# Attention of the second tower: one head after another, or two heads side by side

## What is computed

```python
def diff_attend(q1, q2, k1, k2, v, lam):
    scale = DIFF_QK_DIM ** -0.5
    p1 = jax.nn.softmax(jnp.einsum('bqhd,bkhd->bhqk', q1, k1).astype(jnp.float32) * scale, axis=-1)
    p2 = jax.nn.softmax(jnp.einsum('bqhd,bkhd->bhqk', q2, k2).astype(jnp.float32) * scale, axis=-1)
    p = (p1 - lam * p2).astype(v.dtype)
    return jnp.einsum('bhqk,bkhv->bqhv', p, v)

def gqa_attend(q, k, v):
    B, Q, H, d = q.shape
    qg = q.reshape(B, Q, GQA_KV_HEADS, GQA_GROUP, d)
    s = jnp.einsum('bqgrd,bkgd->bgrqk', qg, k).astype(jnp.float32) * (d ** -0.5)
    p = jax.nn.softmax(s, axis=-1).astype(v.dtype)
    return jnp.einsum('bgrqk,bkgd->bqgrd', p, v).reshape(B, Q, H, d)

def attn_heads(q1, q2, qb, k1, k2, va, kb, vb, lam, lam_init, subln):
    B, Q = q1.shape[:2]
    oa = rms_norm_2(diff_attend(q1, q2, k1, k2, va, lam), subln) * (1 - lam_init)
    ob = gqa_attend(qb, kb, vb)
    return jnp.concatenate([oa.reshape(B, Q, -1), ob.reshape(B, Q, -1)], axis=-1)
```

## Time and profile before

| | us |
|---|---|
| median of three runs | 3231.71 |
| span of the profiled execution | 3245.1 |
| TensorE busy in it | 2922.6 |
| VectorE busy | 1840.6 |
| ScalarE busy | 1181.5 |
| GpSimd busy | 1162.3 |
| attention of the second tower, first score matmul to output projection | 257.9 |

### The profile page before, as it was taken

The page is one execution under the profiler, slowest core; times in us unless marked ns, Lnnn a source line. Parts: engine busy times, 40 slices in busy tenths (PEclk is TensorE's granted clock), DMA queues, the critical chain, the costliest instruction groups (busy, mean ns, idle before and its releaser), DMA issues.

```text
span 3245.1 us, 37354 instructions
## 1 busy us (share of the span) xinstructions
PE 2922.6 (90%) x13432; PEld 2251.8 (69%) x13432; DVE 1840.6 (57%) x2520; ACT 1181.5 (36%) x1710; POOL 1162.3 (36%) x545
## 2 busy tenths in 40 slices
PE   0989898999999789989999699999899999789997
PEld 0855476888888645567777487555688878668886
DVE  7849677554646438589999753744541331454133
ACT  3325523121222425432223532354452433355242
POOL 5289212323332284134444221000344443234442
PEclk9999999999999899999999898899999999899999
DMA  6310033322323110135554231100233232123332
GB/s 245 131 65 1 1 120 120 119 100 100 123 97 131 57 65 1 40 136 181 172 179 167 101 133 39 59 1 15 77 96 97 97 104 76 55 78 97 98 97 72
DMA packets 82261, 303.56 MB, mean 94 GB/s; under 512 B 8928, under 2 KB 10464, under 8 KB 81248
## 3 DMA queue, kind: packets, MB, share of 16 engines
q1 hardware_dynamic: 81856, 298.42, 27.1%
q10 hardware_dynamic: 288, 3.55, 0.3%
HBM read 299.83 MB, written 2.10 MB: 93 GB/s over the span
## 4 chain that ended last, share of the span: by engine, by line
PE 74%; DVE 13%; issue 6%; ACT 4%; POOL 1%; DMA 1%; DVEq 0%; SPq 0%; ACTq 0%; POOLq 0%
PE psum L1401 21%; PE psum L1521 14%; PE psum L1118 9%; PE psum L1542 7%; PE psum L1217 5%; PE psum L1191 4%; PE psum L1156 2%; PE psum L1203 2%; PE psum L1138 2%; DVE product_scratch L1685 2%; DVE rstd L1628 2%; PE psum L1309 1%; DVE scratch L1973 1%; DVE scratch L1611 1%; DVE in_lo L1602 1%
## 5 line engine op out<-in xcount | busy, mean ns | idle before, releaser
L537 POOL TENSOR_TENSOR w_lo<-w_raw,w_hi 128x1024 fp32r<-128x1024 f32 x346 | 879.1, 2541 | 2025.6 <-ACT w_hi L611 2025.6
L611 ACT ACTIVATE w_hi<-w_raw 128x1024 fp32r<-128x1024 f32 x346 | 366.6, 1060 | 1222.1 <-PE psum L1401 488.1
L1690 DVE CUSTOM_DVE_ANT_0 mod_w<-mod_w,conditions 128x1024 f32<-128x1024 f32 x176 | 345.2, 1961 | 5.7
L1665 DVE SCALAR_TENSOR_TENSOR residual<-psum,modulation,residual 128x512 f32<-128x512 f32 (+1 forms) x168 | 111.7, 685 | 345.8 <-PE psum L1542 156.9
L1521 PE MATMUL psum<-in_hi,w_hi 128*128 128x512 f32 x672 | 261.6, 389 | 2.0 <-DVE small_w L2132 1.0
L1521 PE MATMUL psum<-in_hi,w_lo 128*128 128x512 f32 x672 | 261.4, 389 | 0.0
L1521 PE MATMUL psum<-in_lo,w_hi 128*128 128x512 f32 x672 | 261.4, 389 | 0.0
L1401 PE MATMUL psum<-hidden_hi,w_hi 128*128 128x512 f32 (+1 forms) x768 | 237.6, 364 | 25.5 <-DVE hidden_lo L1959 25.1
L1191 PE MATMUL psum<-mixer_space 96*128 96x384 f32 (+2 forms) x544 | 225.9, 542 | 17.0 <-DVE mixer_space L1865 10.3
L1401 PE MATMUL psum<-hidden_hi,w_lo 128*128 128x512 f32 (+1 forms) x768 | 236.3, 362 | 0.0
L1401 PE MATMUL psum<-hidden_lo,w_hi 128*128 128x512 f32 (+1 forms) x768 | 234.5, 360 | 0.0
(11 more groups left out here) (237 smaller groups left out, 5759.5 us busy)
## 6 DMA issues: line engine op xcount, KB each, us to landing
w_raw<-stream_dram SPq DMA_DIRECT2D x346, 512.0 KB, 3.8
mod_w<-mods_dram SPq DMA_DIRECT2D x176, 512.0 KB, 3.5
mixer_space<-mods_dram SPq DMA_DIRECT2D x12, 512.0 KB, 10.7
small_w<-small_w_dram SPq DMA_DIRECT2D x2, 2048.0 KB, 11.2
in_hi_space<-dft_x_dram SPq DMA_DIRECT2D x2, 2048.0 KB, 9.1
residual<-tokens_dram ACTq DMA_DIRECT2D x1, 3072.0 KB, 13.2
conditions<-conditions_dram SPq DMA_DIRECT2D x2, 1024.0 KB, 5.8
in_lo_space<-mods_dram SPq DMA_DIRECT2D x4, 512.0 KB, 9.4
```

The source lines that it names most:

```text
L537: nc.gpsimd.tensor_tensor(wlo[:, (j % 2) * 1024:(j % 2 + 1) * 1024], raw3[:, j, :], whi[:, (j % 2) * 1024:(j % 2 + 1) * 1024].bitcast(F32) ...
L611: nc.scalar.activation(whi[:, (j % 2) * 1024:(j % 2 + 1) * 1024], raw3[:, j, :], ACT.Copy).then_inc(hi_ready, 1)
L1665: last = nc.vector.scalar_tensor_tensor(res3[:, m, s0:s1], bank(2 * (t % 2) + b, c1=s1 - s0), M(block_, chunk, m, 1 - b), res3[:, m, s0:s1 ...
L1690: nc.vector.tensor_tensor_reduce(w_tile, w_tile, cvec[:, 0:D], 1.0, 0.0, ALU.mult, ALU.add, dots[:, q:q + 1]).then_inc(mod_done, 1)
```

## The change

`gqa_plan` becomes `pair_plan`: its steps alternate between an even head (side 0, rows 0-63) and the odd head beside it (side 1, rows 64-127), and a group is two heads at 256 queries. A **pair** d is steps 2d and 2d+1, the two sides of one look. There are 16 differential pairs (first and second looks in turn) and 16 grouped pairs, still 64 steps. Slots, buffers and arithmetic are the same; now side 0 always has banks 0-1 and side 1 banks 2-3, and `pt2` has one buffer per side.

The scores of a pair are issued in alternation, and wait for both exponentials of the pair before. Grouped weighted sums alternate between the sides, into the two halves of bank 6's partitions, so that there are eight evictions of 128 partitions in place of sixteen of 64. Differential ones stay apart. The orders of ScalarE and VectorE go by pairs. The modulation tiles stand one in each of the pairs 0 to 11, after the maxima of the next pair. The head norms start at pairs 10, 13, 18 and 21, and the inverse root and the gain are now both in the pair after the start.

```diff
-SUB_AT, SUB_STEP = 33, 7
+SUB_AT = (10, 13, 18, 21)
+DIFF_PV = 8
...
+            for c in range(2):
                 for q0 in (0, 256):
...
+                    group(c, q0, "diff", [(c, c), (2 + c, 2 + c)])
+            for c in range(4):
+                for q0 in (0, 256):
+                    group(c, q0, "gqa", [(4 + c, 4)])
...
+            pair_exp(0)
+            pair_exp(1)
+            for d in range(n_pairs):
+                before = pair_steps[2 * d - 2] if d else None
+                if d and before["last"]:
+                    pair_hi(pair_groups[before["group"]], 0)
+                if d >= 2 and pair_steps[2 * d - 4]["last"] and pair_steps[2 * d - 4]["post"] == "second":
+                    pair_hi(pair_groups[pair_steps[2 * d - 4]["group"]], 1)
+                for i in (2 * d, 2 * d + 1):
+                    pair_ev(i)
+                if d + 1 < n_pairs:
+                    for i in (2 * d + 2, 2 * d + 3):
+                        pair_exp(i)
+                sub_norm(d)
...
+            def pair_scores(d):
+
+                if d:
+                    pe.wait_ge(sa["exped"], 2 * d)
+                for b in (0, 1):
+                    for i in (2 * d, 2 * d + 1):
+                        st = pair_steps[i]
+                        mm = pe.matmul(bank(2 * (i % 2) + b, c1=384), st["q"],
+                                       st["k"][:, 384 * b:384 * b + 384], start=True, stop=True)
+                        if b:
+                            mm.then_inc(sa["scores"], 1)
...
+                for k in range(6):
+                    for side in range(2):
+                        mm = pe.matmul(bank(6, 64 * side, 64 * side + 64, 0, 256),
+                                       v2[:, k, 512 + 64 * side:576 + 64 * side], pt2[side][:, k, :],
+                                       start=(k == 0), stop=(k == 5))
+                mm.then_inc(sa["pv"], 1)
+
+            pair_scores(0)
+            for d in range(n_pairs):
+                pair_turn(2 * d)
+                if d + 1 < n_pairs:
+                    pair_scores(d + 1)
+                if d and pair_steps[2 * d - 1]["last"] and pair_steps[2 * d - 1]["post"] == "second":
+                    pair_pv_diff(2 * d - 1)
+                pair_turn(2 * d + 1)
+                if pair_steps[2 * d]["last"]:
+                    if pair_steps[2 * d]["post"] == "second":
+                        pair_pv_diff(2 * d)
+                    else:
+                        pair_pv_gqa(2 * d)
...
+            for d in range(n_pairs):
+                for i in (2 * d, 2 * d + 1):
+                    pair_weigh(i)
+                if d and pair_steps[2 * d - 1]["last"] and pair_steps[2 * d - 1]["post"] == "plain":
+                    pair_lo(pair_groups[pair_steps[2 * d - 1]["group"]])
+                if d + 1 < n_pairs:
+                    for i in (2 * d + 2, 2 * d + 3):
+                        pair_max(i)
+                if d < MOD_ATT:
+                    mod_tile(m0 + d, d, False)
+                if d == MOD_ATT:
+                    mod_out(m0, MOD_ATT, group, False)
+                sub_norm(d)
```

More of the change, by code:

```diff
@@ new lines, in pair_plan, with group @@
+        def pair_plan():
+            steps, groups = [], []
+            def group(tile, q0, kind, looks):
+                g = len(groups)
+                groups.append(dict(tile=tile, q0=q0, kind=kind))
+                for j in range(2):
+                    for n, (qt, kt) in enumerate(looks):
+                        for side in range(2):
+                            r = slice(64 * side, 64 * side + 64)
+                            steps.append(dict(
+                                group=g, half=j, side=side, last=j == 1 and n == len(looks) - 1,
+                                post="plain" if len(looks) == 1 else ("first", "second")[n],
+                                q=q2[r, qt, q0 + j * P:q0 + (j + 1) * P], k=k2[r, kt, :]))
+            for c in range(2):
+                for q0 in (0, 256):
+                    group(c, q0, "diff", [(c, c), (2 + c, 2 + c)])
+            for c in range(4):
+                for q0 in (0, 256):
+                    group(c, q0, "gqa", [(4 + c, 4)])
+            turns = 0
+            for st in steps:
+                st["t"] = None
+                if st["post"] != "first":
+                    st["t"] = turns
+                    turns += 1
+            pvs = 0
+            for gr in groups:
+                gr["pv"] = [pvs, pvs + (gr["kind"] == "diff")]
+                pvs = gr["pv"][1] + 1
+            return steps, groups
@@ L983, in _ @@
             nc.scalar.activation(coef[:, 0:2], bank(7, c1=2), ACT.Exp).then_inc(s2["lam"], 1)
[L985 to L995, removed]
+            sa = att[2]
@@ new lines, in pv_free, with pair_pv_diff @@
+            def pv_free(e):
+                if e:
+                    pe.wait_ge(sa["pv_hi"], e)
+                if e > DIFF_PV:
+                    pe.wait_ge(sa["pv_lo"], e - DIFF_PV)
+            def pair_pv_diff(i):
+                st = pair_steps[i]
+                gr = pair_groups[st["group"]]
+                h = 2 * gr["tile"] + st["side"]
+                pe.wait_ge(sa["ev"], st["t"] + 1)
+                pv_free(gr["pv"][st["side"]])
+                for k in range(6):
+                    mm = pe.matmul(bank(6, c1=256), v2[:, k, h * P:(h + 1) * P], pt2[st["side"]][:, k, :],
+                                   start=(k == 0), stop=(k == 5))
+                mm.then_inc(sa["pv"], 1)
```

157 lines of the change are left out of this document (103 added, 54 removed).

## The result

Four runs of the changed kernel took 3247.74 to 3258.60 us, median 3252.18; four of the kernel before, beside them, 3229.77 to 3233.35, median 3231.37. The ratio is 1.0065, with a 95% interval of 1.0051 to 1.0080: **slower by 20.8 us, 0.65%**. The forecast was 3255 us.

A forecast was written before the change was run, and what follows sets the result against it. TensorE, busy 90% of the span, was taken as the bound. Stage 279 us at clock 0.75, 21 over 257.9, plus 2 for the projection: +23 on 3231.7, so 3255 us; own range 3241 to 3268, full range 3228 to 3287.

The forecast's parts named there:

- What bounds the stage, and what the loop loses: Second tower's attention: TensorE bounds it; pairs fill both score slots, so scores can't run ahead; 211 us before head norms.
- The four spacings at the full clock: Scores to next pair's scores: first look 4.9, second look with tile 7.2, grouped without weighted sum 5.8, with it 6.8 us.
- Full overlap of the array's row halves: Two heads' scores cost 1.49 us instead of 2.98; with paired weighted sums, TensorE's list shrinks by 69 us.
- Rival 1: Scores overlap less, a pair taking five lengths: stage 295 us at clock 0.75, kernel 3271; chance 0.09.
- The modulation tile on the path: On VectorE in second looks, the tile stands ahead of the weighting and adds 1.20 us, in six pairs.
- Rival 4: Some loop item, say the modulation tile, is hidden; gain and loss cancel within 6 us; chance 0.08.
- The head norms: Four times, VectorE's gain waits for ScalarE's root ahead of both weightings: 25 us for all four at full clock.
- The clock: TensorE pauses in every pair, so the stage's mean granted clock is taken as 0.75, against 0.85 before.
- mixing of 236 and 342 us: New stage's layout at full clock and with every TensorE item doubled, mixed by mean clock: 279 us at 0.75.
- break-even at 0.86: Mean stage clock at which the new stage equals the old; faster above it.
- Rivals 2 and 3: Clock falls to 0.6: stage 314, kernel 3290 us, chance 0.09; clock stays 0.95: stage 243, kernel 3217, chance 0.12.
- The projection's cold start: The output projection after the stage begins at the low clock about half the time: 2 us added.

The follow-up runs named there:

- e9: Kernel before with only the grouped weighted sums of two heads in pairs, and head norms' inverse roots replaced by a copy: 3209.06 us, ratio to before 0.9933.
- e12: Kernel of e6 with the head norms' inverse roots replaced by a copy: 3216.80 us, ratio to before 0.9954.
- e2: Changed kernel with both heads' scores on array rows 0-63, the even head's computed twice: 3330.84 us in its one execution.
- e3: Changed kernel with the even head's score matmuls issued before the odd head's, not in alternation: 3255.87 us, ratio to before 1.0059.
- e5: Changed kernel with VectorE's twelve modulation tiles moved ahead of the next pair's maxima: 3243.80 us, ratio to before 1.0040.
- e1: Changed kernel with VectorE's gain and remainder of each head norm one pair later: 3226.59 us, ratio to before 0.9975.
- e4: Changed kernel with one unused matmul added at the end of pairs without a weighted sum, away from the norms: 3239.47 us, ratio to before 1.0017.
- e6: Changed kernel with the edits of e1 and e5, head norms at pairs 10, 14, 18, 22 and ScalarE's copy later: 3216.23 us, ratio to before 0.9959.
- e7: Kernel before with only the grouped weighted sums of two heads in pairs, scores still one step ahead: 3225.95 us, ratio to before 0.9981.

## Why the prediction was right

- **What bounds the stage, and what the loop loses.** Right. TensorE's list carried the stage before, the one-step lead fed it, and the pairs lost the lead. The four spacings at the full clock were forecast as 4.9, 7.2, 5.8 and 6.8 us; the trace has 5.03, 7.12, 5.80 and 6.81, in the five of 31 pairs that ran wholly at the full clock. That the lead was lost is read from these spacings and from e9 beside e12. No kernel that pairs the scores and keeps a lead ran, so its share of the 81 us is not measured.
- **Full overlap of the array's row halves**, taken from the column case of rows 6. Right: 1.56 us for eight records, and e2 and e3 show it from both sides. Rival 1, five record lengths a pair, is out by the 1.56 us, and by e3. The TensorE list was to shrink by 69 us at the full clock; busy time fell by 64, at a lower clock. The Trainium skill ("TensorE: Matmul & The Clock Gate", Part 3) lets matmuls start only in list order; e3's pair, at 1.57 us with one head wholly ahead of the other, disagrees with it. The Trainium skill ("TensorEngine Tiling (Array Packing)", Key Properties) says that tiles operate independently, and e3 agrees. Rows 6, which the prediction set against list order, decide less: the two projection records belong to one matmul, and the weighted sum starts after the first of them.
- **The modulation tile on the path.** Right in place, too large in size: the sum has 1.2 us for each of six at the full clock, the pairs of e5 show 0.8. Its 9.9 us hold what the clock gave back. Rival 4 is out.
- **The head norms.** Right in place, and one wait of two: VectorE idles 4.02, 5.00, 5.16 and 5.17 us ahead of the gains, about 4 was forecast. The waits ahead of the remainders, 7.4 us, are in no term of the sum. The size was 25 us at the full clock, some more at 0.75; e1, which removes both kinds, gained 27.3. That the size fits is therefore partly luck.
- **The clock.** 0.75 was taken, 0.77 granted. The prediction's own mixing of 236 and 342 us gives 275.3 at 0.77; the stage took 275.0, where 279 was forecast. The 0.75 was a choice between rows, not worked out from them, and that it lay so near is in part luck. The 10 us at the low level that it read from rows 2 are no rule: in the same trace the clock came back after 6.8 us (from 2155.97) and after 3.4 (from 2217.41). The break-even at 0.86 could not be tried for the changed kernel alone: e4 reached 0.85 with its 30 extra records and took 261.3, 3 us over before. Rivals 2 and 3 are out for the kernel as it was changed.
- **The projection's cold start**, 2 us. Wrong: the 50.6 us behind the stage have the same 194 matmul records and a clock of 0.95 for 0.96.
- **The sum.** +21 for the stage, +17.1 measured; +23 for the kernel, +20.8 measured. The 3.7 us between the stage's share and the kernel's are within the drift outside the stage and stay unplaced. Two figures of the working do not follow from their own terms, and neither moves the forecast: a second look without the tile adds up to 6.0, not 6.1, and a clock of 0.70 gives 3266, not 3268.

What the prediction did not see is how near the other sign was. It took the costs on VectorE as parts of the new order; they belong to placements within it, and e6 takes off 37.5 us with a few offsets and the place of one call.

## What to carry to other kernels

Two float32 matmuls of 64 rows on different halves of the array took as long as one, in whatever order they were listed (1.56 and 1.57 us for eight records, 1.55 for four of one head). But when both fill the only two slots, nothing is left to compute ahead with, and the time goes into the chain of the other engines. So pair first what needs no score slot, as e7 and e9 do: e9's grouped part took 114.5 us, that of the pairs without roots 133.8.

After an order is changed, look first at each wait that now stands ahead of several others on an in-order engine. Here a gain and a remainder, each placed one iteration too early on VectorE, cost 27 us in four places, more than the change lost.

And do not count what TensorE saves as time saved before you have read its idle time: here 64 us less work came with 81 us more waiting.

## What was not expected of the hardware

- More TensorE work made a kernel faster: 30 more records of 128x512 matmuls raised the stage's clock from 0.77 to 0.85 and took 13 us off the kernel (e4).
- Leaving work out does not have to help: e12, without the four roots, has a clock of 0.83 in its one profile where e6 has 0.87, and the same time (3216.8 and 3216.2 us).
- Of row halves listed one head after the other (e3) neither head's records wait for the other's; the eight take 1.57 us against 1.56 in alternation.
